# Softmax attention: the transposes of the job two steps back stand between the mask products and the values, no longer behind the values

## The reference, cut to what matters

```python
s = jnp.einsum('bqgrd,bkgd->bgrqk', qi, ki).astype(jnp.float32) * scale
s = jnp.where(mask, s, NEG)
p = jax.nn.softmax(s, axis=-1)          # with sinks: a further term in the denominator
return jnp.einsum('bgrqk,bkgd->bqgrd', p.astype(vi.dtype), vi)
```

## Time and profile before

| | us |
|---|---|
| median of 3 runs | 2772.98 |
| lowest, highest | 2769.99, 2773.42 |
| span of the profiled execution | 2773.0 |
| NSA attention in it | 299 to 358 |
| SWA attention in it | 794 to 827 |
| hybrid attention in it | 1317 to 1340 |

### The profile page before, as it was taken

How to read it: one execution, slowest core, us unless ns; L and a number is a source line. 1 busy time by engine, 2 the same in 40 slices (tenths; PEclk the granted TensorE clock), 3 DMA queues, 4 the chain that set the end, 5 groups by cost and what they waited for, 6 DMA issues and landing times.

```text
span 2773.0 us, 43755 instructions
## 1 busy us (share of the span) xinstructions
PE 2713.9 (98%) x17288; PEld 2402.6 (87%) x17288; DVE 1872.2 (68%) x2051; ACT 1245.2 (45%) x1594; POOL 637.9 (23%) x519
## 2 busy tenths in 40 slices
PE   8999999999999999999999999999999999999998
PEld 7987789999979999998799888888888878888887
DVE  6785765578867877665666657666766767665765
ACT  4443454444444444444444454434534454444443
POOL 5863310068635961000100100000000420000000
PEclk9999999999999999999999999999999999999999
DMA  7654145557526765433354435535653435533552
GB/s 296 255 205 155 47 163 192 198 220 276 189 90 245 275 235 213 182 144 122 129 204 182 164 116 208 203 130 181 229 195 138 144 140 225 200 133 109 210 207 91
DMA packets 126992, 501.89 MB, mean 181 GB/s; under 512 B 11168, under 2 KB 12480, under 8 KB 93488
## 3 DMA queue, kind: packets, MB, share of 16 engines
q1 hardware_dynamic: 112768, 450.40, 44.7%
q0 software_dynamic: 14128, 50.18, 5.1%
HBM read 499.48 MB, written 1.06 MB: 181 GB/s over the span
## 4 chain that ended last, share of the span: by engine, by line
PE 89%; DVE 6%; ACT 2%; issue 1%; DMA 1%; POOL 1%; DVEq 0%; SPq 0%; POOLq 0%; ACTq 0%
PE duo L1257 8%; PE duo L1242 8%; PE duo L1343 8%; PE duo L1243 8%; PE duo L1347 8%; PE duo L1351 8%; PE duo L1240 8%; PE duo L1256 4%; PE duo L1678 3%; PE duo L1679 3%; PE duo L1683 3%; DVE in_lo L366 1%; PE duo L2225 1%; PE duo L2224 1%; PE duo L2223 1%
## 5 line engine op out<-in xcount | busy, mean ns | idle before, releaser
L366 DVE TENSOR_TENSOR in_lo<-ring_in,in_hi 128x2048 fp32r<-128x2048 f32 x295 | 698.9, 2369 | 345.2 <-ACT in_hi L359 344.8
L359 ACT CAST in_hi<-ring_in 128x2048 fp32r<-128x2048 f32 (+1 forms) x293 | 555.9, 1897 | 243.9 <-PE duo L1683 130.8
L366 DVE TENSOR_TENSOR down_lo<-ring_down,down_hi 128x1024 fp32r<-128x1024 f32 (+1 forms) x196 | 338.9, 1729 | 29.2 <-ACT down_hi L359 29.2
L1432 ACT CAST hid_hi<-act 128x256 fp32r<-128x256 f32 (+1 forms) x196 | 93.3, 476 | 418.3 <-DVE act L1518 347.9
L359 ACT CAST down_hi<-ring_down 128x1024 fp32r<-128x1024 f32 (+1 forms) x196 | 260.4, 1329 | 44.2 <-PE duo L1351 44.2
L1343 PE MATMUL duo<-down_hi,hid_hi 128*128 128x512 f32 x984 | 256.9, 393 | 1.3 <-ACT hid_hi L1432 1.3
L1347 PE MATMUL duo<-down_lo,hid_hi 128*128 128x512 f32 x984 | 253.6, 389 | 0.0
L1351 PE MATMUL duo<-down_hi,hid_lo 128*128 128x512 f32 x984 | 253.1, 389 | 0.0
L1240 PE MATMUL duo<-feat,in_hi 128*128 128x512 f32 x1024 | 250.9, 395 | 0.0
L1242 PE MATMUL duo<-feat,in_hi 128*128 128x256 f32 (+1 forms) x1014 | 243.1, 282 | 5.3 <-ACT in_hi L359 3.4
L1243 PE MATMUL duo<-feat,in_hi 128*128 128x256 f32 (+1 forms) x1014 | 240.9, 280 | 0.0
(11 more groups left out here) (532 smaller groups left out, 5554.0 us busy)
## 6 DMA issues: line engine op xcount, KB each, us to landing
ring_in<-in_ffn_in SPq DMA_DIRECT2D x196, 1024.0 KB, 6.5
ring_down<-in_ffn_down SPq DMA_DIRECT2D x132, 512.0 KB, 3.6
ring_down<-in_ffn_down SPq DMA_DIRECT2D x64, 1024.0 KB, 4.8
mod_w<-in_w_ada POOLq DMA_DIRECT2D x72, 512.0 KB, 5.1
ring_in<-in_sb_w_qkv SPq DMA_DIRECT2D x24, 1024.0 KB, 5.2
ring_in<-in_conv_w_in SPq DMA_DIRECT2D x12, 1024.0 KB, 5.2
ring_in<-in_gla_w_in SPq DMA_DIRECT2D x12, 1024.0 KB, 5.1
ring_in<-in_nsa_w_in SPq DMA_DIRECT2D x10, 1024.0 KB, 5.0
```

Source lines behind the costliest of these rows:

```text
L359: act.copy(hi[:, s, 0:n], raw[:, s, 0:n]).then_inc(hi_ready.sem, 1)
L366: dve.tensor_tensor(lo[:, s, 0:n], raw[:, s, 0:n], hi[:, s, 0:n].bitcast(F32), ALU.subtract).then_inc(lo_ready.sem, 1)
```

## The change

In `Attention.tensor` the call `_turn_next(pe, step - LAG)` is made for all steps from LAG to n + LAG - 1 at one place, ahead of the values. Before, it stood ahead of them only from step n on and behind them in the steps below n. The other engines' programs are the same, word for word.

```diff
             if step == n and self.out:
                 pe.wait_ge(k.att_exp.sem, self.exp0 + n - 1)
                 self.out.tile(pe, 0, 0, 0)
-            if n <= step < n + self.LAG:
+            if self.LAG <= step < n + self.LAG:
                 self._turn_next(pe, step - self.LAG)
             if step > self.LAG:
                 i = step - self.LAG - 1
...
                 self._values(pe, i)
-            if self.LAG <= step < n:
-                self._turn_next(pe, step - self.LAG)
```

## The result

| | changed | before, beside it |
|---|---|---|
| median (7 runs each) | 2780.98 us | 2772.98 us |
| lowest, highest | 2777.37, 2786.51 | 2769.99, 2777.55 |
| ratio, 95% interval | 1.0024 [1.0013, 1.0034] | |
| profiled execution, its span | 2777.37, 2775.5 us | span 2773.0 us |

I had forecast 2774.7 us in a range of 2769.0 to 2779.0. The changed kernel took 2780.98 us: slower than forecast and outside the range. Yet the trace shows the steps doing almost exactly what I had worked out, so the question of this study is where the other microseconds are.

A forecast was written before the change was run, and what follows sets the result against it. PE, busy in 98% of the span, was taken to bound the kernel. NSA +1.3, SWA +0.4 and hybrid 0.0 us gave +1.7 us on 2773.0 us: 2774.7 us, with a range of 2769.0 to 2779.0.

The forecast's parts named there:

- What bounds the kernel: Whole kernel: PE is busy in 98% of the span, so only changes to PE's own sequence count.
- the places of the waits: PE waits for POOL in NSA steps 5, 7, ..., 15 and SWA steps 4 and 6.
- Term 1: NSA and SWA steps: fewer changes of matmul form, saving 0.11 us per even and 0.13 us per odd step, 2.2 us whole.
- The allowance for a slow first instruction: After a change of matmul form: 0.02 us more saved in an even step, 0.04 us in an odd one.
- Term 2: Moved transposes wait for POOL's scaling: 3.0 us lost in NSA; 1.2 us in SWA, less 0.25 us of vanished L1989 waits.
- Release: The third transpose starts 0.06 us after POOL's end, 3.28 us after the previous job's reduction in NSA.
- Term 3: DVE's copy starts up to 0.8 us earlier, nobody waits for it; the shift passes whole behind NSA and SWA; hybrid 0.0 us.
- Rivals A and B: A: no POOL wait, gain stays, 2770.8 us, 12%. B: a wait in each of 19 steps, 2779.7 us, 5%.
- Rival C: New waits in NSA lower PE's clock: 2791 us if once per pair of steps, 2777.4 us for one spell; 4%.
- The sum's base and the range: Terms added to the 2773.0 us span; 2772 to 2777.5 for the forecast's own case, 8 in 10 within 2769.0 to 2779.0.

The follow-up runs named there:

- nsa_short_pool: Kernel before with the new order in NSA alone and POOL's scaling cut to the first 16 columns of each piece: ratio 0.9986, -3.5 ± 1.1 us.
- same_third: The kernel before, unchanged, in a third series with its own trace: ratio 1.0007, +1.4 ± 1.2 us, without one execution of 10240 us.
- moved_again: The changed kernel run once more, unaltered, against the kernel before: ratio 1.0009, +3.8 ± 1.1 us.
- nsa_long_pool: Kernel before with the new order in NSA alone and one more small POOL instruction ahead of each scaling there: ratio 1.0001, +1.75 ± 1.5 us.

## Why the prediction was wrong, point by point

**What bounds the kernel; the places of the waits: right.** PE sets the pace, the waits come in every second step, and mask to transposes takes 0.34 us (317.50 to 317.84; 0.35 forecast).

**Term 1, right in kind, a little small.** The even step went from 2.89 to 2.74 us, 0.15 us saved where I took 0.11. The allowance for a slow first instruction was meant as 0.02 us; the transposes as a group now last 0.82 us and took 0.87 before, so it is 0.05. (The Trainium skill, "TensorEngine Tiling (Array Packing)", "Key Properties", says that changing the tiling mode drains TensorE; nsa_short_pool agrees, in which no wait for POOL is left and a pair with fewer changes of form is 0.33 us shorter.) In one place the count of changes was wrong: in the last step of NSA and of SWA the transposes used to stand ahead of the output projection, which has their form, and now the values do. There nothing is saved. NSA's step 15 grew by 0.59 us (10.64 to 11.23 us up to the projection behind the attention), the other odd steps by 0.40.

**Term 2, right.** A pair takes 6.51 us against 6.52. The odd step grew to 3.77 us where 3.36 + 0.50 - 0.13 = 3.73 was worked out. Release: third transpose 0.05 us after POOL's end (0.06 taken). From step 4 on NSA came out at 6 x 0.26 = 1.56 us by the working, 1.68 measured. SWA from step 4 stood at 1.2 - 4 x 0.11 - 0.25 = +0.5, measured +0.20. The values there had waited for DVE's L1989 three times and not less: mask to values took 0.69 us in steps 5, 6 and 7 of before (810.74 to 811.43 in step 5) and 0.55 us in step 4 (807.73 to 808.28), so 0.42 us of waits vanished and not 0.25. Three steps save 0.15 us and not 0.11, the last saves nothing. What is left of the gap, 0.13 us, is in the two waits, which came out shorter (0.41 us idle each, 0.55 worked out). That the whole attentions add up so well, NSA +1.57 where 1.3 was forecast and SWA +0.31 where 0.4 was, is thus in part luck: small errors took each other back.

**Term 3, right.** Nobody waits for the earlier copy, the shift passes whole to the end of both attentions, and the hybrid's end still waits 2.68 us for DVE. One small thing I hadn't seen: the transposes now also reach ACT's L3217 early once, 0.5 us in the group above, in SWA's step 3, where it takes back that step's gain (3.61 us from scores to scores, 3.54 in same_third). With this long step ahead of it POOL is done in time for step 4, and the waits for it fall in steps 5 and 7.

**Rivals A and B: excluded by the trace.** The waits are there, and only in each second step; also where SWA's steps are nearly equal (moved_again), PE waits in 4 and 6 alone, 0.15 us each.

**Rival C: excluded in the form given.** I feared that the new waits would bring the lower clock inside NSA. The stretch of the earlier trace rows in the changed kernel:

```profile
302.60:306.40 3.80, 1.91 (x13) 1.31 (x14) 3.23 (x11) 2.51 (x13) 1.63 (x4) 1.00 0.00 0
306.40:311.80 5.40, 5.40 (x46) 4.31 (x47) 3.65 (x9) 3.32 (x16) 3.25 (x8) 1.00 0.01 3
316.00:350.00 34.00, 32.21 (x271) 24.34 (x270) 25.95 (x68) 19.99 (x94) 17.78 (x44) 1.00 0.01 2
```

Clock 1.00 with PE busy 32.21 of 34.00 us and a wait in each pair. The trace of nsa_long_pool, with longer waits, has 1.00 in the same stretch too, and its kernel as a whole measured +1.75 ± 1.5 us, not more than the +3.35 us in its steps. (The Trainium skill, "TensorE: Matmul & The Clock Gate", "A second HAM failure mode: psum-queue depth-cycling", tells of a kernel whose clock swung with short idles between its groups of matmuls; in this stretch it stayed at 1.00.) The rows also take back what I built rival C on: ahead of 306.40 PE was busy 1.84 of 3.80 us in one trace and 1.91 in the other, and what followed ran at 0.50 in one and at 1.00 in the other. A half-clock stretch seen once in one trace isn't a consequence that can be counted on.

**The sum's base and the range: here it failed.** The step was "Around the forecast lie the three runs' own spread (2769.99 to 2773.42, 3.4 us)", and before it the sum was made on 2773 us as if that were the kernel's time. (That the span equals the median is an accident too: each execution's time is 1.9 us over its span, as 2777.37 and 2775.5 us above.) The experiments ran the kernel before 161 times beside theirs: mean 2775.9 us, standard deviation 3.3 us, from 2768.9 to 2785.2. Three runs that lie within 3.4 us are a lucky draw, and their median has a standard error of about 1.25 x 3.3 / 1.73 = 2.4 us (worked out for a normal scatter), a median of seven 1.6 us. The distance from 2774.7 to 2780.98 us then splits so:

| | us |
|---|---|
| base: 2775.9 instead of 2773.0 | +2.9 |
| steps: +1.9 instead of +1.7 | +0.2 |
| rest not in the steps, 3.9 - 1.9 (± 0.7) | +2.0 |
| scatter of this median of 7 (remainder) | +1.2 |

And the ratio of 1.0024 overstates the change: of its 8.0 us, 3.9 are the change, 2.9 the low draw of before, 1.2 the high draw of the changed kernel. The interval of [1.0013, 1.0034] holds 3.9 us (1.0014) only at its edge. The chance of 91% for "within 0.2%" rested on the same narrow scatter; by the longer series it is the right answer for the kernels (1.0014), not for what one comparison of seven runs shows.

**Open.** The 2.0 ± 0.7 us of rest, of which some 1.2 us go with a lower clock. I had argued only with time in the steps and gave the clock 4% as one spell in NSA. I did not ask whether time at the lower clock elsewhere, some 44 us in the trace of before (0.992 over 2773.0 us), could shift by a few microseconds with the change, and the runs don't settle what would make it do so.

## What to carry to other kernels

Before sizing an effect of a few microseconds, look at the kernel's own scatter: multiply one minus the mean granted clock by the span. That is more than the low clock costs (here 1.7 us for each 0.001 of clock, where this count gives 2.8), but if it is many times the effect, three runs are no base and their spread no range. With dozens of runs, compare them at equal clock too: it took the scatter of one execution here from 3.5 to 2.0 us. Measure small reorderings between the same two instructions in the trace, where they repeat to some hundredths of a microsecond, and take the time of the whole kernel only from dozens of runs.

When a consumer is moved earlier, compute the producer's release from the reduction that starts its chain, as in term 2, and look for independent work of the same form to stand in the gap: here the opener ahead of the transposes turns +1.7 us into -0.9 us.

## What the runs showed of the hardware that I had not expected

- The kernel's executions differ by up to 16 us (2768.9 to 2785.2) with the same instructions, and the longer ones are those with the lower mean clock (correlation -0.81 over 161). The 20 traces have from 28 to 70 us at 1.2 GHz, in five to twelve stretches, in places that change from one execution to the next.
- The same idle time ahead of a stretch, 1.9 of 3.8 us busy, was followed by 0.50 in one execution and 1.00 in another.
- At half clock PE was busy for all of 3.40 us (801.0 to 804.4 us of before), and the attention around it became only 0.6 us longer than in same_third.
- A wait of 0.4 us in each 6.5 us, with PE busy 95% (32.21 of 34.00 us), left the clock at 1.00 throughout.
